# The second head's choice is made between the first head's dots on VectorE

## The reference, cut to what matters

```python
def peer_ffn(h, wq, keys1, keys2, u_tab, v_tab):
    q = (h @ wq).reshape(n, PEER_HEADS, 2, PEER_HALF)
    s1 = jnp.einsum('thc,nc->thn', q[:, :, 0], keys1)
    s2 = jnp.einsum('thc,nc->thn', q[:, :, 1], keys2)
    t1, i1 = lax.top_k(s1, PEER_TOPK)
    t2, i2 = lax.top_k(s2, PEER_TOPK)
    cand_s = (t1[..., :, None] + t2[..., None, :]).reshape(n, PEER_HEADS, 256)
    cand_i = (i1[..., :, None] * PEER_N_KEYS + i2[..., None, :]).reshape(n, PEER_HEADS, 256)
    top_s, pos = lax.top_k(cand_s, PEER_TOPK)
    idx = jnp.take_along_axis(cand_i, pos, axis=-1)
    gate = jax.nn.softmax(top_s, axis=-1)
    act = jax.nn.gelu(jnp.einsum('td,thkd->thk', h, u_tab[idx]))
    return jnp.einsum('thk,thkd->td', gate * act, v_tab[idx])
```

## Time and profile before

| what | value |
|---|---|
| median of 3 runs | 2374.2 us (2372.78 to 2378.0) |
| the profiled execution: its own time | 2372.37 us |
| the profiled execution: span of the core | 2370.7 us |
| mean granted TensorE clock | 0.971 |
| busy, share of the span: TensorE, VectorE, GpSimd, ScalarE | 84%, 70%, 54%, 13% |
| DMA traffic | 794.62 MB, mean 335 GB/s |

### The profile page before, as it was taken

One profiled execution on the slowest core, in us unless ns is written; L12 is line 12 of the kernel. 1 busy time (PEld: TensorE's weight loads), 2 busy tenths in 40 slices (PEclk: granted clock), 3 DMA queues, 4 the chain that ended last, 5 costly groups with the idle time before them and its releaser, 6 DMA issues.

```text
span 2370.7 us, 30558 instructions
## 1 busy us (share of the span) xinstructions
PE 2002.9 (84%) x10334; PEld 838.8 (35%) x10334; DVE 1667.3 (70%) x3942; ACT 300.5 (13%) x655; POOL 1270.4 (54%) x1559
## 2 busy tenths in 40 slices
PE   5999999988889996888898779999777777777677
PEld 4444444443555676532233123333111111111111
DVE  3797798875654447866666786667787998677753
ACT  2112222232112112111000100101000000000000
POOL 0342233214443304666667666767675777777774
PEclk7999999979999998999999999999999999999999
DMA  8786676689777638999999999999999999999996
GB/s 308 253 285 199 213 237 210 200 303 323 248 251 260 228 131 290 376 407 405 403 405 406 401 363 401 398 404 409 411 409 353 385 409 409 409 409 404 409 409 273
DMA packets 264362, 794.62 MB, mean 335 GB/s; under 512 B 33296, under 2 KB 64756, under 8 KB 263576
## 3 DMA queue, kind: packets, MB, share of 16 engines
q0 software_dynamic: 191008, 680.63, 76.3%
q1 hardware_dynamic: 73216, 112.20, 13.4%
HBM read 781.60 MB, written 11.11 MB: 334 GB/s over the span
## 4 chain that ended last, share of the span: by engine, by line
DMA 21%; POOL 16%; PE 9%; issue 7%; DVE 6%; ACT 1%; PEldq 0%; ACTq 0%; PEld 0%; POOLq 0%; DVEq 0%
DMA arena<-in_peer_v,arena 20%; POOL arena L986 16%; PE banks L1632 6%; DVE arena L2864 2%; DMA arena<-in_peer_u,arena 2%; PE banks L1606 1%; PE banks L1011 1%; PE banks L1663 0%; PE banks L1583 0%; ACT L1946 0%; DVE arena L2807 0%; DVE arena L2810 0%; PE banks L1648 0%; DVE arena L2567 0%; DVE arena L2570 0%
## 5 line engine op out<-in xcount | busy, mean ns | idle before, releaser
L1632 PE MATMUL banks<-arena 128*32 128x512 f32 x2048 | 927.6, 604 | 255.7 <-DMA arena<-in_peer_v,arena 251.4
L2864 DVE CUSTOM_DVE_ANT_0 arena<-arena,banks 128x1024 f32<-128x1024 f32 x496 | 602.1, 1216 | 299.3 <-DMA arena<-in_peer_u,arena 294.9
L986 POOL DMA_INDIRECT arena<-in_peer_u,arena x520 | 501.4, 964 | 267.2 <-issue 142.6
L986 POOL DMA_INDIRECT arena<-in_peer_v,arena x520 | 492.1, 946 | 244.7 <-issue 126.8
L1632 PEld LDWEIGHTS banks<-arena 128*32 128x32 f32 x2048 | 182.2, 109 | 917.1 <-DMA arena<-in_peer_v,arena 522.5
L1011 PE MATMUL banks<-arena 128*128 128x128 f32 (+6 forms) x1512 | 377.4, 406 | 9.1 <-DMA arena<-in_peer_wq 2.7
L968 POOL DMA_DIRECT2D arena<-in_cache_k x256 | 137.4, 537 | 329.3 <-DVE arena L2136 227.5
L1700 ACT ACTIVATE arena<-banks 128x512 f32<-128x512 f32 (+12 forms) x360 | 154.3, 429 | 1188.3 <-PE banks L1663 350.1
L1011 PEld LDWEIGHTS banks<-arena 128*128 128x128 f32 (+2 forms) x1512 | 236.0, 191 | 152.0 <-issue 135.6
L968 POOL DMA_DIRECT2D arena<-in_cache_v x256 | 137.3, 536 | 229.4 <-PE banks L1300 174.0
L2131 DVE TENSOR_TENSOR arena<-arena 128x512 f32<-128x512 f32 x256 | 175.2, 685 | 23.5 <-DMA arena<-scratch_queries 19.1
(11 more groups left out here) (301 smaller groups left out, 1626.3 us busy)
## 6 DMA issues: line engine op xcount, KB each, us to landing
arena<-in_cache_k POOLq DMA_DIRECT2D x256, 256.0 KB, 3.4
arena<-in_cache_v POOLq DMA_DIRECT2D x256, 256.0 KB, 4.4
arena<-in_w_ada SPq DMA_DIRECT2D x12, 2048.0 KB, 12.7
arena<-in_w_in SPq DMA_DIRECT2D x10, 2048.0 KB, 12.8
arena<-in_peer_wq SPq DMA_DIRECT2D x16, 1024.0 KB, 17.2
arena<-in_peer_u,arena POOLq DMA_INDIRECT x520, 12.5
arena<-in_peer_v,arena POOLq DMA_INDIRECT x520, 12.5
scratch_gates<-arena SPq DMA_DIRECT2D x16, 256.0 KB, 3.6
```

The lines of the kernel that those rows point to most:

```text
L986: nc.gpsimd.indirect_dma_start(gathered[:, j, :], None, tables[kind[0]][:, :], OFF(ap=index, axis=0)).then_inc(row_in[j], 16)
L1632: ins = mm(acc[u][32 * j:32 * (j + 1), :], spread[:, n % 2, b, :], gathered_row(("v", t, x))[:, 512 * u:512 * (u + 1)], start=x < 4, stop= ...
L2864: release(nc.vector.tensor_tensor_reduce(out=row, in0=row, in1=h2[:, t, :] if x < WIDE_AT else h2_wide, scale=1.0, scalar=0.0, op0=MUL, op ...
```

## The change

VectorE no longer runs `choose(0, 1)` as one block before the loop of heads. It is the first entry of head 0's side chain, and head 0 takes three steps after each dot in place of two. The pause of 8 steps in that chain is dropped. ScalarE's `gate_exp(1)`, which waits for that choice, moves from before its loop to x = 5 in it, behind p of head 2 for tile 1 and ahead of the scores of head 2 for tile 0.

```diff
@@ block.scalar
             next(first)
             widen(0)
-            gate_exp(1)
             for x in range(NT * SLOTS + LAG):
                 now[0] = x
                 next(first, None)
                 next(rest, None)
+                if x == 5:
+                    gate_exp(1)
@@ block.vector
             dve.wait_ge(blocks_in, 16)
             run(choose(0, 0))
             first_tile(1)
-            run(choose(0, 1))
             now = [0]
             rest = second_group(now)
             for n in range(HEADS):
@@
                 if n:
                     side = [gelu_first(n - 1), gate_sums(n), gelu_last(n - 1)]
                 else:
-                    side += [pause(8), index_columns(0)]
-                steps = 2
+                    side = [choose(0, 1), gate_sums(0), index_columns(0)]
+                steps = 2 if n else 3
```

## The result

| | before | after |
|---|---|---|
| median of 6 runs each | 2374.28 us (2370.06 to 2378.0) | 2383.53 us (2380.28 to 2385.97) |
| profiled execution: own time, span | 2372.37, 2370.7 us | 2381.22, 2379.6 us |
| mean granted TensorE clock | 0.971 | 0.967 |

The ratio is 1.0036, with a 95% interval of 1.0024 to 1.0047: slower by 5.7 to 11.2 us. The forecast was 2378.1 us in a range of 2370 to 2384.

What follows compares the result with a forecast made beforehand. DMA engines bound over half the span, a stretch whose start is set by T (head 2's scores reach VectorE) and work to dot 24. Terms -1.14 + 1.13 + 3.9 = +3.9 us gave 2378.1 us, range 2370 to 2384.

Steps and rivals of the forecast that it cites:

- rival B: `wq0_2`'s load alternates packets with gathers and takes up to 17.1 us: +8.8 us, 2383.0 us; chance 0.12.
- The head start of the dots: VectorE's dot 0 starts 8.95 us earlier, but VectorE still idles until head 2's scores arrive: worth nothing.
- One dot fewer behind T: Eight dots, not seven, precede VectorE's wait for head 2's scores, shortening its work from there to dot 24: -1.14 us.
- The table load ahead of the scores' copy: On ScalarE, `gate_exp(1)`'s table load and exponential delay the copy of head 2's scores that VectorE awaits: +1.13 us.
- The load of `wq0_2` behind three gathers: u12, u13 and u14, issued ahead of TensorE's weight load, go first and delay it 3 x 1.31: +3.9 us.
- 11 to 13.5 us: Sign for the forecast: `wq0_2` takes this long from issue to landing, and TensorE waits for it until about 926.
- 8 to 9 us: Time of `wq0_2`'s load from issue to landing that would show rival A right.
- rival A: `wq0_2`'s load is not hindered and the two small terms cancel: no effect, 2374.2 us; chance 0.20.
- all four gathers: By the skill's rule of queues in turn, four gathers precede the load's last packet: term 5.2 us, sum 5.2.
- Three steps per dot: Head 0's three side steps after a dot bring VectorE's dots closer at the block's end, dot 24 unmoved: 0.
- an earlier `index_columns(1)`: Coming behind dot 12, not 14, perhaps removes GpSimd's 3.82 us pause before v0; counted as 0.
- Rival C: Total transfers set the end and the head start is kept, up to 5.6 us gained: 2368.6 us; chance 0.12.

Runs made afterwards that it cites:

- gate in front: `gate_exp(1)` put back ahead of ScalarE's loop: in the changed kernel ratio 1.0021; with u12 also held to the load's issue 1.0003, to its landing 1.0010.
- held kernels: Changed kernel with gather u12 waiting for `wq0_2`'s issue (1.0010, 1.0002) or landing (1.0011); with `gate_exp(1)` also ahead of ScalarE's loop 1.0003 and 1.0010.
- third profile: Changed kernel run again without an edit, beside the kernel before on a chip where that takes 2374.86 us: 2380.66 us, ratio 1.0024.
- series 4: Last series of runs, with changed, held and before kernels on one chip; the kernel before takes 2374.86 us there.
- first two profiles of the changed kernel: Changed kernel unedited, in the original comparison (2383.53 us, 1.0036) and run again on a slower chip (2453.97 us, 1.0023).
- series 2 and 3: Two series of follow-up runs on slower chips, where the kernel before takes 2448.82 and 2445.22 us; only ratios are compared across series.
- with u12 held: Kernel before with only gather u12 made to wait until `wq0_2` has landed: 2447.67 us, ratio 1.0007.
- gate moved alone: Kernel before with only `gate_exp(1)` moved to x = 5 in ScalarE's loop, the choice left in front: 2449.50 us, ratio 1.0002.
- kernel before (2): Kernel before run again without an edit, on a slower chip: 2446.43 us, ratio 0.9989.

## Why the prediction was right, and where it was not

The sign was right and the range holds the time, but with luck. The forecast's +3.9 us (0.16%) lay inside what cannot be told from no change; the measured 0.24 to 0.36% lies above that, which had been given a chance of 0.32. The 2383.53 us lie outside the forecast's own range, 2374 to 2381.5, and inside the outer one only because that had been stretched to 2384 for rival B, whose mechanism the runs do not show. The steps, with the mean of three profiles of either kernel:

**The head start of the dots is worth nothing: right.** VectorE was idle 6.26 to 8.41 us at T. A time in front of a wait that another engine ends brought nothing.

**One dot fewer behind T, -1.14 us: right in kind, -0.78 measured** (32.42 to 31.64 in every profile of either kind). The missing 0.36 us is not attributed.

**The table load ahead of the scores' copy, +1.13 us: right as a delay, not seen in the time.** The copy starts 1.84 us behind the previous copy's start, where it had been 0.67, so +1.17. The rule of the Trainium skill (ScalarE: Activation LUTs, "What ACT_TABLE_LOAD costs") with its drain of 1.38 us behind the load does not hold here: the exponential starts at 939.72, 0.01 us after the load's end. I had added this term as though the alternative were free. It is not, as the gate in front showed: once the choice is spread, ScalarE would stand 3.41 us.

**The load of `wq0_2` behind three gathers, +3.9 us: the mechanism is shown, but the base of the sum was wrong.** Against the held kernels the load is late by 9.0 - 5.6 = 3.4 us in the mean. In the third profile, the only one with the gathers about where the forecast had them, it is late by 9.6 - 5.6 = 4.0, three gathers of 1.31. But against the kernel before it is late by only 9.0 - 7.2 = 1.7 us, because there one part of it lands late in two of three profiles. I had read the 8.3 us of the earlier trace rows as the undisturbed load, so the 11 to 13.5 us that I forecast, and 8 to 9 us as the sign of rival A, stood on a wrong base.

What I left out filled the gap. From TensorE's first product to T pass 1.5 us more, 1.2 of it the table load; the products also ran slower behind the wait (5.47, 5.47 and 6.60 us against 5.36, 3.82 and 5.47). And SP's issue comes 0.7 us later behind the norm, which is not the change's doing. The products ahead of the issue took 6.4 and 6.5 us at a mean granted clock of 0.58 and 0.57 in the first two profiles of the changed kernel, 5.8 us at 0.65 in the third, and 5.4, 5.4 and 5.8 us at 0.70, 0.70 and 0.65 in those of before; the stretch at 1.2 GHz had begun ahead of the first changed instruction (granted clock 0.50 from 906 to 910 us in the first profile, whose norm ends at 910.5).

The Trainium skill (DMA: Bandwidth & Descriptors, "Queues, rings and completion order") has the engines take their queues in turn; by that all four gathers would stand ahead, 5.2 us. The trace does not agree: in series 4 the load moved nothing in the first 2 us, and it was 4.0 us late.

So the path from the norm to T grew by 0.7 + 1.7 + 1.5 = 3.9 us, and to dot 24 by 3.9 - 0.8 = 3.1. The forecast had 5.0 and 3.9.

**Three steps per dot, 0: right, within the scatter.** From dot 24 to dot 64 pass 107.5 to 108.9 us after and 107.3 to 109.6 before. The guess in this step that an earlier `index_columns(1)` removes GpSimd's 3.82 us ahead of v0 was wrong: the pause is still there, 3.65 us, and what ended it is now GpSimd's own issue.

**Rival A** was refuted by the held kernels: the load is hindered, and undoing that undoes the loss. **Rival B** named a time near the measured one, 2383.0, with a load of up to 17 us that takes turns with the gathers; no load took more than 9.6, and no turns are seen. **Rival C** fell with the sign.

**What stays open is 2 to 5 us.** The measured losses were 9.3, 5.6 (taken from 0.23%) and 5.8 us; the part behind the norm explains 3 to 4. In the profiles from chips on which before takes 2374 us, what is left from the norm to the end is 1464.8 and 1466.5 us before, 1469.1 and 1470.0 changed, 1462.5 and 1463.1 held. By that the held kernels should win 2.8 us; in time they are even (-0.7 us, interval -2.4 to +3.3). Both gaps would close if every kernel with the changed VectorE part lost some 2 us ahead of the norm, and in these profiles the norm ends at 905.9 and 906.3 before, 908.0 and 908.8 held, 910.5 and 912.3 changed. In series 2 and 3 that order is not there (before 908.7 and, with u12 held, 911.1; gate moved alone 916.8; changed 912.7 and, with the gate in front, 912.0; held 907.5 to 910.0). Nothing of the change runs in that place, and no run isolates it. It is not settled.

## What to carry to other kernels

Before letting an engine free buffers earlier, list every transfer that the freed buffers trigger and every plain load due in that window: the gathers went ahead of one 1 MB load and delayed the whole chain behind it, while their own data was not due. Where the early start is wanted anyway, one wait that holds the first early gather until the load has been issued takes the loss back, though here it brought no gain over the kernel before. And an "undisturbed" duration read from one profile should be checked against a second one before it serves as the base of a term.

## What the runs showed that was not expected

- The same load takes 5.4 us or up to 8.3 us in unchanged text: in profiles of the kernel before TensorE waited 2.72, 0 and 2.40 us for it, with u12 issued 2.0 to 2.3 us behind it each time. The difference is one of its 16 landings.
- A plain load issued behind gathers got almost nothing until they were moved: first packet after 3.1 us behind three of them, after 1.0 to 1.1 us with none issued early.
- A wait of TensorE cost more than itself, because the granted clock fell. The 32 products took 3.82 us with no wait and 3.84 us after one of 0.48, at a clock of 1.00; 5.36 to 5.47 us at 0.69 to 0.70 after waits of 1.8 to 3.3 us; 5.83 at 0.64 after 4.49; and 6.60 at 0.56 after 3.96. Duration times clock is 3.7 to 3.8 us in each. The first row is of the kernel before (2), the second of the changed kernel (4):

```profile
922.30:926.12 3.82, 3.82 (x36) 3.82 (x36) 3.07 (x8) 2.57 (x5) 2.80 (x4) 1.00 1.03 369
930.48:937.08 6.60, 6.60 (x34) 6.60 (x35) 4.61 (x15) 0.28 (x1) 3.75 (x4) 0.56 0.72 227
```

- GpSimd stands 3.65 to 3.83 us ahead of the first gather of v rows in every profile, whatever is moved around it.
- The place ahead of the change scattered between profiles: `choose(0, 0)` started anywhere from 884.5 to 895.5 us, and the norm behind it took 21.3 us in twelve profiles and 23.1 and 23.4 in two, both of the changed kernel, where the products ahead of it had a mean granted clock of 0.81. A comparison of two single profiles can be off by several us for that reason alone; counting from a fixed event just ahead of the change removes most of it. It does not remove all: in those two profiles the gathers had run ahead of the norm's end, and the load met fewer of them.
